# Sums of squares on TensorE, quarter tiles for the samples, and one add moved, in a two-layer decoder step

## What is computed

```python
def rmsnorm(x, g):
    y = x * lax.rsqrt(jnp.mean(x * x, axis=-1, keepdims=True) + NORM_EPS) * g
def short_conv_mixer(h, prev, w_in, w_dw, w_out):
    b_gate, c_gate, v = jnp.split(h @ w_in, 3, axis=-1)
    uc, st = causal_dwconv(c_gate * v, prev, w_dw)
    return (b_gate * uc) @ w_out, st
def conv_ffn(h, prev, w_up, w_dw, b_dw, w_down):
    g, u = jnp.split(h @ w_up, 2, axis=-1)
    gc, st = causal_dwconv(g, prev, w_dw)
    return (jax.nn.silu(gc + b_dw) * u) @ w_down, st
# layer 0: short conv; layer 1: stick-breaking attention (no softmax)
# every layer: x += mixer(rmsnorm(x)); x += conv_ffn(rmsnorm(x)); at the end one more rmsnorm
```

## Time and profile before

| what | value |
|---|---|
| median of three executions | 2708.8 us (2707.02 to 2710.52) |
| the profiled execution's own time | 2711.09 us |
| its span, first to last instruction | 2709.3 us |
| PE busy | 2609.6 us, 96% |
| DVE busy | 1475.8 us, 54% |
| POOL busy | 725.2 us, 27% |
| ACT busy | 539.9 us, 20% |
| mean granted clock of PE | 0.983 |

### The profile page before, as it was taken

How to read it: one execution, slowest core, us unless ns; L and a number is a source line. 1 busy time by engine, 2 the same in 40 slices (tenths; PEclk the granted TensorE clock), 3 DMA queues, 4 the chain that set the end, 5 groups by cost and what they waited for, 6 DMA issues and landing times.

```text
span 2709.3 us, 40755 instructions
## 1 busy us (share of the span) xinstructions
PE 2609.6 (96%) x16774; PEld 2472.5 (91%) x16774; DVE 1475.8 (54%) x1512; ACT 539.9 (20%) x1077; POOL 725.2 (27%) x415
## 2 busy tenths in 40 slices
PE   7999999999999999989999999789999999999996
PEld 7999999999999999988888888459999999999995
DVE  7333455444444455587777777533754444444446
ACT  4000221000000000144444444320300000000013
POOL 3333333223332233221111111013322233333333
PEclk9999999999999999999999999899999999999998
DMA  4111111111111111121111111631111111111111
GB/s 137 47 42 45 48 47 40 47 47 47 43 44 47 47 47 40 50 111 40 40 40 40 44 44 40 220 102 47 39 40 47 47 47 47 47 47 47 47 42 65
DMA packets 60330, 149.04 MB, mean 55 GB/s; under 512 B 5522, under 2 KB 28818, under 8 KB 60178
## 3 DMA queue, kind: packets, MB, share of 16 engines
q1 hardware_dynamic: 51298, 123.86, 14.2%
q10 hardware_dynamic: 8880, 22.85, 2.2%
HBM read 128.91 MB, written 17.78 MB: 54 GB/s over the span
## 4 chain that ended last, share of the span: by engine, by line
PE 86%; DVE 8%; issue 2%; ACT 2%; POOL 1%; DMA 0%; SPq 0%; DVEq 0%; POOLq 0%; ACTq 0%
PE bank L474 26%; PE bank L478 25%; PE bank L477 25%; PE bank L706 3%; PE bank L646 3%; PE bank L679 2%; DVE a_lo L1285 1%; DVE h_lo L1155 1%; DVE total L1164 1%; DVE x L1293 1%; DVE y L1283 1%; ACT a_hi L836 1%; POOL y_rows L466 1%; PE bank L770 1%; PE bank L804 1%
## 5 line engine op out<-in xcount | busy, mean ns | idle before, releaser
L474 PE MATMUL bank<-h_hi,w_hi 128*128 128x352 f32 x3648 | 1197.1, 328 | 29.8 <-DVE ext L1272 8.8
L478 PE MATMUL bank<-h_hi,w_lo 128*128 128x352 f32 x3648 | 1177.6, 323 | 0.0
L477 PE MATMUL bank<-h_lo,w_hi 128*128 128x352 f32 x3648 | 1176.6, 323 | 0.0
L450 POOL CAST w_hi<-raw 128x1024 fp32r<-128x1024 f32 x196 | 217.9, 1112 | 1937.7 <-PE bank L474 1894.3
L474 PEld LDWEIGHTS bank<-h_hi,w_hi 128*128 128x128 f32 x3648 | 690.2, 189 | 42.5 <-issue 31.2
L477 PEld LDWEIGHTS bank<-h_lo,w_hi 128*128 128x128 f32 x3648 | 691.7, 190 | 0.7 <-issue 0.4
L478 PEld LDWEIGHTS bank<-h_hi,w_lo 128*128 128x128 f32 x3648 | 691.3, 190 | 0.0
L452 POOL TENSOR_TENSOR w_lo<-raw,w_hi 128x1024 fp32r<-128x1024 f32 x196 | 488.1, 2490 | 15.7
L1293 DVE TENSOR_TENSOR x<-x,bank 128x1056 f32<-128x1056 f32 x174 | 216.2, 1251 | 290.8 <-PE bank L478 290.8
L474 PE MATMUL bank<-a_hi,w_hi 128*128 128x352 f32 x1056 | 343.9, 326 | 11.7 <-DVE x L1293 11.7
L477 PE MATMUL bank<-a_lo,w_hi 128*128 128x352 f32 x1056 | 342.1, 324 | 0.0
(11 more groups left out here) (111 smaller groups left out, 1757.7 us busy)
## 6 DMA issues: line engine op xcount, KB each, us to landing
raw<-weights SPq DMA_DIRECT2D x196, 512.0 KB, 3.4
page_k<-cache_k SPq DMA_DIRECT2D x16, 512.0 KB, 7.0
page_v<-cache_v SPq DMA_DIRECT2D x16, 512.0 KB, 6.1
x_spill<-x ACTq DMA_DIRECT2D x8, 528.0 KB, 6.1
k_out<-k_t ACTq DMA_DIRECT2D x8, 528.0 KB, 2.7
v_out<-v_t ACTq DMA_DIRECT2D x8, 528.0 KB, 2.9
x<-x_spill ACTq DMA_DIRECT2D x8, 528.0 KB, 7.4
y_out<-y_rows ACTq DMA_DIRECT2D x3, 1408.0 KB, 5.3
```

The costliest lines, as they stand in the source:

```text
L450: nc.gpsimd.tensor_copy(w_hi[ring][:, :], raw[slot][:, :]).then_inc(w_high, 1)
L474: mm = nc.tensor.matmul(o, w_hi[w][:, c0:c0 + P], hi, start=first, stop=False)
L477: nc.tensor.matmul(o, w_hi[w][:, c0:c0 + P], lo, start=False, stop=False)
L478: return nc.tensor.matmul(o, w_lo[w][:, c0:c0 + P], hi, start=False, stop=last)
```

## The change

Six edits. (1) In both FFN loops the first `add_x` of a round moves ahead of the subtraction of the second `ffn_chunk` (`between`). (2) `last_mean` is issued inside the second tile, behind its chunk `k == 2`; in the short-conv stage inside the third tile. (3) There ACT copies the first gate (`copy_gate(0)`) between the squares of the first norm, and its loop is written out. (4) For the two norms behind FFNs, the squares go in a ring of 12 blocks, and PE sums four of them at a time (`sum_four`): each by a product with 32 columns of `mean`, into its own quarter of the partitions; after two such groups ACT copies the bank to `quad`, and `fold_mean` multiplies it by a matrix of 1/32. DVE sums nothing there. The ring of product banks is six instead of seven, and the first QKV chunks use other banks. (5) The samples' products go by 32 columns: a query chunk only meets the 32 columns of its heads, and value halves likewise; result, copy, transposes and picks halve. (6) At the end DVE computes `x * gain * rstd` in one step for 0, 4 and 8 chunks of the three blocks, POOL the others, and each block is stored in two halves, by ACT's and by SP's queue.

```diff
-RING, MEAN_BANK = 7, 7
-FIRST_BANK = [3, 4, 5, 2, 0, 1, 2, 0, 1]
-MEANS_IN = ((), (KC * 2 - 2, BLOCKS - 4))
+RING, QUAD_BANK, MEAN_BANK = 6, 6, 7
+FIRST_BANK = [0, 1, 2, 3, 4, 5, 0, 1, 2]
+QUADS_IN = (6, 10, 14, 18, 22)
+MEANS_IN = ((16,), (14, 22))
+COPY_AT, ROOT_AT = (12, 20), 17
-Y_BY_DVE = (0, 0, 5)
+Y_BY_DVE = (0, 4, 8)
...
             def linear(tile, ring, s, fill, midway=None):
...
+                    if k == 2 and midway is not None:
+                        midway()
...
+                    if c in QUADS_IN:
+                        sum_four(nth, QUADS_IN.index(c))
                     if c in mean_after:
-                        mean_next(nth, mean_after.index(c))
+                        fold_mean(nth, mean_after.index(c))
+            def sum_four(nth, n):
+                pe.wait_ge(squared, SQ_BASE[nth] + 4 * n + 4)
+                if n % 2 == 0 and n:
+                    pe.wait_ge(quad_copied, TJ * (nth // 4) + n // 2)
+                for g in range(4):
+                    mm = nc.tensor.matmul(projected(QUAD_BANK)[32 * g:32 * g + 32, :], mean[:, 0:32], square_of(4 * n + g),
+                                          start=n % 2 == 0, stop=n % 2 == 1, skip_group_check=True)
+                mm.then_inc(quads, 1)
+            def fold_mean(nth, j):
+                pe.wait_ge(quad_copied, TJ * (nth // 4) + j + 1)
+                pe.wait_ge(root_made, TJ * nth + j)
+                nc.tensor.matmul(projected(MEAN_BANK), fold[:, :], quad[:, :], start=True, stop=True).then_inc(mean_full, 1)
...
                 project(first, n, FIRST_BANK[n], None, H_QKV if n < TJ else None)
-                if 1 <= n <= TJ:
-                    mean_next(2, n - 1)
+                if n == 0:
+                    fold_mean(2, 1)
+                    sum_four(2, QUADS - 1)
+                if n == 1:
+                    fold_mean(2, 2)
...
+                for page in range(PAGES):
+                    for r in range(0, P, 32):
+                        b, g = r // 64, r // 32 % 2
+                        mm = nc.tensor.matmul(o_s[bp % 2][r:r + 32, :], w_ts[:, page, r:r + 32],
+                                              page_v[2 * (bp % 2) + b][:, page, 512 * g:512 * g + 512], start=False,
+                                              stop=page == PAGES - 1, skip_group_check=True)
...
+                    high(2, c % KC, c // KC)
+                    square_in_ring(2, c)
+                    if c in COPY_AT:
+                        copy_sums(2, COPY_AT.index(c))
+                    if c == ROOT_AT:
+                        root(2, 0, MEAN_BANK)
+                root(2, 1, MEAN_BANK)
+                copy_sums(2, 2)
+                root(2, 2, MEAN_BANK)
...
+            for c in range(BLOCKS):
+                add_block(B_FFN1, c)
+                if c == ROOT_AT + 1:
                     invert(4, 0)
                 for j in range(1, TJ):
                     invert(4, j)
+                    dve.wait_ge(rstd_made, TJ * 4 + j + 1)
+                    for f in range(Y_BY_DVE[j]):
+                        V.scalar_tensor_tensor(y_rows[:, f, tokens(j)], x[:, f, tokens(j)], gain[:, 4, f:f + 1],
+                                               rstd[:, tokens(j)], ALU.mult, ALU.mult).then_inc(y_made, 1)
...
                 V.tensor_tensor(yy, yy, result(s), ALU.mult).then_inc(taken[s], 1)
+                if between is not None:
+                    between()
                 dve.wait_ge(a_high, m - (KC - 1))
```

More of the change, by code:

```diff
@@ L216, in build @@
         eps = sb("eps", [P, 1])
+        fold = sb("fold", [P, P])
         bias_now = [sb(f"bias_now{n}", [P, 1]) for n in range(2)]
@@ L262, in build @@
         v_new = sb("v_new", [NS, D])
-        o_rows = sb("o_rows", [P, D])
+        o_rows = [sb(f"o_rows{n}", [P, D // 2]) for n in range(2)]
         beta_s = [sb(f"beta_s{n}", [P, PAST + NS]) for n in range(2)]
@@ L286, in build, with square_of @@
         attended = out[0][:, 1, :]
-        o_s = out[0][:, 0:2, :].rearrange("p a b -> p (a b)")
+        o_s = [out[0][:, n, :] for n in range(2)]
+        o_turned = [spare[:, n, :] for n in range(2)]
+        def square_of(c):
+            n = c % SQUARE_RING
+            return (square + c_gate)[n // TJ][:, tokens(n % TJ)]
         def sem(name):
@@ L371, in build, with y_ready @@
         block = ctx.enter_context(nc.Block())
+        def y_ready(engine, j):
+            engine.wait_ge(y_by_pool, sum(Y_BY_POOL[:j + 1]))
+            if Y_BY_DVE[j]:
+                engine.wait_ge(y_made, sum(Y_BY_DVE[:j + 1]))
         @block.sync
@@ L440, in _ @@
                 load_tile(early + n, n % RAW)
+            for j in range(TJ):
+                y_ready(sp, j)
+                sp.dma_start(y_out[KC // 2:KC, :, tokens(j)].rearrange("f p t -> p f t"),
+                             y_rows[:, KC // 2:KC, tokens(j)]).then_inc(stored, 16)
         @block.gpsimd
@@ L460, in _ @@
                 split_tile(n, n % RAW, n % SPLIT, n // RAW + 1)
-            for j in range(TJ):
+            for j in range(TJ - 1):
                 pool.wait_ge(rstd_made, TJ * 4 + j + 1)
                 for f in range(Y_BY_DVE[j], KC):
-                    pool.wait_ge(y_gained, KC * j + f + 1)
+                    pool.wait_ge(y_gained, sum(Y_BY_POOL[:j]) + f - Y_BY_DVE[j] + 1)
                     nc.gpsimd.tensor_tensor(y_rows[:, f, tokens(j)], y_rows[:, f, tokens(j)], rstd[:, tokens(j)],
@@ L492, in last_mean, with linear @@
                 mean_of(nth, 2, 6)
-            def linear(tile, ring, s, fill):
+            def linear(tile, ring, s, fill, midway=None):
                 pe.wait_ge(w_split, tile + (RAW + 1))
@@ L547, in up @@
                     else:
-                        linear(tile + n, (ring0 + n) % SPLIT, s, fill)
-                    if n == 1 and norm is not None:
-                        last_mean(norm)
+                        linear(tile + n, (ring0 + n) % SPLIT, s, fill,
+                               (lambda: last_mean(norm)) if n == 1 and norm is not None else None)
             def down(tile, ring0, k0, name, trip, slot, group, early_release):
@@ L614, in ffn @@
                           MEANS_IN[layer])
-            pe.wait_ge(made, 1)
+            pe.wait_ge(made, 3)
             def sc_in(trip):
@@ L829, in _ @@
             ffn(1)
-            mean_next(4, 2)
+            sum_four(4, QUADS - 1)
+            fold_mean(4, 2)
         @block.scalar
@@ L972, in _ @@
             act_op(bias_r[:, 1:2], bias_r[:, 0:1], scale=-1.0).then_inc(negated, 1)
[L973 to L986 removed]
+            for m in range(KC):
+                if m:
+                    copy_gate(m)
+                n, k = m % 2, 3 * m + 1
+                s = (k + 1) % 2
+                act.wait_ge(taken[s], FREE["sc_in"][s] + k // 2 + 2)
+                samples(m, n, st_sc[:, m, :, :], new_sc[:, m, :])
             act.wait_ge(smp_full, 4 * KC)
@@ L1146, in _ @@
             V.memset(eps[:, :], EPS).then_inc(made, 1)
+            V.memset(fold[:, :], 1.0 / 32).then_inc(made, 1)
             for n in range(2):
                 V.memset(ext[n][:, 0:CW - 1], 0.0).then_inc(made, 1)
-            def wide(t):
-                return t.rearrange("p (a b) -> p a b", a=TJ)
             def low(nth, f, j):
@@ L1264, in conv, with ffn_chunk @@
                 last.then_inc(convolved, 1)
-            def ffn_chunk(m, par, chunk, layer, k, trip, slot):
+            def ffn_chunk(m, par, chunk, layer, k, trip, slot, between=None):
                 name = f"ffn{layer}"
@@ L1297, in ffn, with up @@
                 m0 = M_FFN[layer]
-                def up(m, chunk, k0, trip, slot):
+                def up(m, chunk, k0, trip, slot, between=None):
                     for p in range(2):
-                        ffn_chunk(m + p, p, chunk + p, layer, k0 + 2 * p, trip, slot)
+                        ffn_chunk(m + p, p, chunk + p, layer, k0 + 2 * p, trip, slot, between if p else None)
                 def down(k0, trip):
-                    for f in range(KC):
+                    for f in range(1, KC):
                         add_x(f, name, k0 + f, trip)
@@ L1519, in _ @@
             final_norm()
-            for j in range(TJ):
-                dve.wait_ge(rstd_made, TJ * 4 + j + 1)
-                for f in range(Y_BY_DVE[j]):
-                    dve.wait_ge(y_gained, KC * j + f + 1)
-                    V.tensor_tensor(y_rows[:, f, tokens(j)], y_rows[:, f, tokens(j)], rstd[:, tokens(j)],
-                                    ALU.mult).then_inc(y_made, 1)
 def kernel(**inputs):
```

168 lines of the change are left out of this document (83 added, 85 removed).

## The result

| | before | after |
|---|---|---|
| median of the runs | 2707.9 us (2705.17 to 2710.52) | 2662.8 us (2660.61 to 2664.49) |
| ratio, 95% interval | | 0.9833 [0.9816, 0.985] |
| profiled execution, its span | 2711.09, 2709.3 us | 2660.61, 2658.6 us |
| PE busy | 2609.6 us | 2581.0 us |
| mean granted clock of PE | 0.983 | 0.989 |

The forecast of 2651 was 12 us too low, and 2662.8 lies inside its own range, 2641 to 2663, by 0.2 us only, which is luck. It is also nearer to the 2661 of the rival "draining at each change", so the number by itself decides nothing between them. Between the two profiled executions the spans differ by 50.7 us, against 57.6 in the sum.

What follows compares the result with a forecast made beforehand. PE was taken as the bound, so only its rests, shrinkable work and low clock could give: 14.0 + 13.6 + 4.2 + 6.5 + 18.0 + 1.3 = 57.6 us, from 2711.09 to 2653.5, said as 2651 for timed runs, range 2641 to 2663.

Steps and rivals of the forecast that it cites:

- draining at each change: Rival: PE empties around each 32-column group, 6 us, and samples keep half the clock, 4 us: 2661 us; chance 0.14.
- the sum: Total gain forecast for all six edits, 57.6 us, taken from the profiled execution's 2711.09 us.
- Its 14.0: FFN rounds: 20 PE waits on the first add, 0.70 us each, vanish; bounds 8.6 to 14.0 us.
- 6.8 each: Ahead of each FFN: an earlier third mean saves 4.6 us of wait and 2.2 of low clock.
- 4.2 predicted: Start: earlier gate copy wins about 5.1 us, less 0.9; bounds 2 and 6.
- the place I named: Fourth tile of the start: a new PE wait of 2.1 us on DVE, its bank free near 55.
- the 0.9 that I had taken off: Start: deduction from about 5.1 us for the chance of another low-clock stretch.
- 6.1 of 6.5: Behind FFN 0: 12.1 us recoverable, less 4.5 for six groups and 0.6, gives 7.0; 6.5 was taken.
- a late first group at 0.6: Behind FFN 0: 0.6 us added because the first group's squares come a little late and further blocks queue.
- 18 predicted: Samples: products by 32 columns end them near 1790 instead of 1808; bounds 4 and 24.3 us.
- 24.3 - 18: Samples: 24.3 us is the upper bound with no wait on pages, 18 the forecast with waits.
- its term: End and final norm: last store at 2707.8 against 2709.3, gain 1.3 us; bounds 3 slower to 5 faster.

Runs made afterwards that it cites:

- the one-column products at the up tiles: Changed kernel with a one-column bf16 product added at the head of each FFN up tile: 2673.15 us, ratio 0.9852.
- the eight: Eight profiles with the changed start and POOL's early split; one tile after the fourth-tile wait they are -0.2 to 2.7 us ahead of before.
- The delayed split: Changed kernel, but POOL splits the fifth weight tile only after DVE's last sum of squares of the first norm: 2659.98 us, ratio 0.982.
- all products in one quarter: Changed kernel, but a group's four squares go to the same 32 partitions, one behind the other: 2683.28 us, ratio 0.9891.
- the add alone: Kernel before with only the first add of a round moved ahead of the subtraction: 2694.71 us, ratio 0.9951.
- the samples alone: Kernel before with only the samples' products by 32 columns (scores, values, halved rows, picks): 2697.48 us, ratio 0.9945.

## Why the prediction was right or wrong

**Edit 1** was right in mechanism and in the waits: all 20 gone, 13.9 us of 14.0, nothing in their place. Its 14.0 took for granted that the rest of the stream keeps its pace, and it does not: in single pairs of profiles the edit is worth 8 to 11, by the averages of three and eight profiles 11. Timed alone it is 12.3, and 14.0 lies inside that interval.

**Edit 2** held: 6.3 and 6.9 for 6.8 each, the same within 0.1 us in every profile of the changed kernel and its variants but that of the one-column products at the up tiles, with no wait and no low clock (0.66 from 418 to 428 before, 1.00 after).

**Edit 3 and the start** failed: 4.2 predicted, nothing in the first profile and about 1 over all, below my bound of 2. I wrote that DVE's sums come 0.7 us later because of the copy. They came 3.4 us later (reciprocals from 46.21, 42.79 before), 2.7 of it through POOL's split, which the earlier third tile had triggered. I had looked at what the faster PE needs next, and not at what it sets free. The wait did come, at the place I named, 57.4 instead of 55, and longer (2.9 for 2.1), and in this execution the clock fell behind it, which cost 2.8:

```profile
56.40:63.20 6.80, 5.80 (x20) 5.84 (x21) 6.65 (x6) 0.54 (x4) 4.26 (x2) 0.50 0.00 0
```

The delayed split shows the first part: with it the sums are over in 4.30, and the fourth tile starts 5.2 and 5.5 us earlier than before instead of 2.6 to 2.9, where I had 5.1. How far the clock fell was the draw of the execution: it cost 2.8 in this one and 1.1 on average over the eight, near the 0.9 that I had taken off. The Trainium skill, "GPSIMD Engine Reference", section "Specifications", names the contention of VectorE and GpSimd where a DVE instruction has two SBUF inputs; the trace agrees: 0.53 us a sum alone, 1.17 and 2.54 the two that met POOL's work.

**Edit 4** held: 6.1 of 6.5. I had a group at 0.75 and a late first group at 0.6; a group took 0.95, some 1.15, and the first group's squares were in time. Six groups cost 1.2 or more over the forecast, the 0.6 and the 0.5 that I had taken off without a reason give that back. That the total came out right is in part luck.

**Edit 5** came out between: 23 in the first pair of profiles, 16 over all, 13.5 timed alone, 18 predicted. The two waits for keys came, 8.1 and 2.8 us in the first profile. Right in the halving (values, scores at full clock). I left out the new keys' products (5.6 us) and undersized the waits and the low clock: 24.3 - 18 leaves 6.3 us for both, and the waits alone are 10.9 to 14.6 in nine profiles, where before had 2.1, with the scores of three pairs at about 0.5 of the clock in the first. Their places were right: PE goes on at 1740.61, which with the 16 us won ahead of it is 1757, and I had said near 1758. How much of the wait is the pages' own transfer and how much the late issue was not separated.

**Edit 6** was 1.6 below its term, within its bounds. (Its own figures, 2709.3 - 2707.8, are 1.5, not 1.3.) DVE's steps of the end, after:

```profile
2639.37 2.35 DVE L1237 RECIPROCAL rstd<-total 128x352 f32<-128x352 f32 x1 [1.00 <-ACT total L888]
...
2641.76 4.84 DVE L1299 SCALAR_TENSOR_TENSOR y_rows<-x,gain,rstd 128x352 f32<-128x352 f32 x4
...
2646.52 2.34 DVE L1237 RECIPROCAL rstd<-total 128x352 f32<-128x352 f32 x1
2648.90 4.06 DVE L1299 SCALAR_TENSOR_TENSOR y_rows<-x,gain,rstd 128x352 f32<-128x352 f32 x8
```

The first reciprocal comes 1.9 us behind PE's last start (2637.48), as reckoned (1.8), the eight products take 4.06 (4.0). The four beside POOL take 4.84 (4.4), and the five groups among the blocks lengthened that stretch by 4.96 us where I had 3.75: this is the price of the groups again, and most of the shortfall. The last group, which waits for the last square, is not on this chain: with all products in one quarter it took 1.7 us more, and the stretch behind the last block stayed at 21.15.

Timed, the add alone gave 12.3 and the samples alone 13.5; by the profiles the means gave 13.2, the stage behind FFN 0 6.1, the start about 1 and the end -0.3. That is 45.8, where 45.1 and 49.2 were measured. The forecast missed by 3 us in the start, some 4 in the samples, 2 in the pace and 1.6 at the end. The first two profiles hid this: a lucky pace before, an unlucky start and lucky samples after.

## What to carry to other kernels

When a change makes one engine reach a point earlier, follow what it sets free there as well as what it waits for next: an engine off the critical path may start its work beside one that is on it, and slow it. One pair of profiles does not price a stage that waits for transfers: here it moved by 6 us with the same code, as much as a whole edit. Small products placed in separate quarters of the array cost a quarter each, plus a fixed 0.36 us here for leaving and re-entering the full-width stream, so they want to be gathered in groups.

## What the runs showed that I had not expected

A stream of fp32r matmuls of 352 columns at full clock runs at 158.9, 160.0 or 161.1 ns a matmul, 1.4% apart, which over the 8472 matmuls of the FFN stages is up to 19 us. It changed only at certain places of the program or at a stop, and a stop of 0.10 us was enough. The full-width bf16 product of one column costs 0.10 to 0.13 us in that stream. The scores with 32 new keys cost under a third of their time when split in quarters (7.9 us to 2.3), although they are products of only 32 columns of data. A sum of squares on DVE that met POOL's subtraction was not slowed by a share but ended 0.38 us after it: 2.54 us instead of 0.53.
